# Six modulation units of layer 1 behind layer 0's last expert, and two result buffers in place of four

## The reference

```
h  = rms(x, attn_norm_g) * (1 + sc1) + sh1          # and hc from the context
y  = attention(h, hc)                               # 8 global heads, 8 local ones with sink
x  = x + g1 * (y @ w_out[l])
h  = rms(x, ffn_norm_g) * (1 + sc2) + sh2
x  = x + g2 * top2_experts(h)                       # 16 experts, in layer 0 for 512 tokens
```

## Time and profile before

| what | us |
|---|---|
| median of 3 runs (lowest to highest) | 1102.76 (1098.95 to 1102.98) |
| the profiled execution, its own time | 1102.94 |
| its span | 1101.0 |
| attention of layer 0 | 156 to 291 |
| experts of layer 0 | 407 to 653 |
| combine | 665 to 691 |
| attention of layer 1 | 765 to 828 |
| experts of layer 1 | 884 to 1095 |

### The profile page before, as it was taken

The page is one execution under the profiler, slowest core; times in us unless marked ns, Lnnn a source line. Parts: engine busy times, 40 slices in busy tenths (PEclk is TensorE's granted clock), DMA queues, the critical chain, the costliest instruction groups (busy, mean ns, idle before and its releaser), DMA issues. The chain is left out here.

```text
span 1101.0 us, 24722 instructions
## 1 busy us (share of the span) xinstructions
PE 934.9 (85%) x9667; PEld 584.8 (53%) x9668; DVE 486.4 (44%) x1375; ACT 299.0 (27%) x678; POOL 51.1 (5%) x71
## 2 busy tenths in 40 slices
PE   4679999899897789999999853799989787999975
PEld 2234465443343755666766533487658654555543
DVE  1416666566513543333333314386871543343422
ACT  3312235455301431111111102423770311122111
POOL 1000000000000001111111113000000000000000
PEclk9889999999898689999999976899999799999988
DMA  8995039879802104999999997302403359999995
GB/s 320 420 395 176 1 136 426 310 283 424 350 5 108 46 1 163 397 418 417 418 418 418 420 413 276 133 1 78 171 1 153 153 236 428 428 428 416 414 430 232
DMA packets 33905, 299.05 MB, mean 272 GB/s; under 512 B 9681, under 2 KB 11105, under 8 KB 16961
## 3 DMA queue, kind: packets, MB, share of 16 engines
q1 hardware_dynamic: 23264, 286.15, 63.4%
q0 software_dynamic: 8880, 12.01, 3.3%
q10 hardware_dynamic: 1712, 0.23, 0.1%
HBM read 289.51 MB, written 16.65 MB: 278 GB/s over the span
## 5 line engine op out<-in xcount | busy, mean ns | idle before, releaser
L730 PE MATMUL bank<-ring,rows_buf 128*32 128x256 f32 x4160 | 248.3, 392 | 54.5 <-DMA ring<-in_w_up_dram 27.4
L730 PEld LDWEIGHTS bank<-ring,rows_buf 128*32 128x32 f32 x4160 | 157.3, 113 | 138.8 <-issue 72.6
L503 PE MATMUL bank<-rows_buf,ring 128*128 128x512 f32 (+1 forms) x320 | 119.3, 528 | 12.5 <-ACT rows_buf L898 6.5
L742 PE MATMUL bank<-ring,rows_buf 128*32 128x256 f32 x2080 | 125.7, 380 | 1.2 <-ACT work L1010 1.2
L503 PEld LDWEIGHTS bank<-rows_buf,ring 128*128 128x128 f32 x320 | 63.2, 198 | 61.7 <-issue 48.2
L742 PEld LDWEIGHTS bank<-ring,rows_buf 128*32 128x32 f32 x2080 | 73.4, 110 | 41.6 <-issue 7.6
L1440 DVE COPY rows_buf<-rows_buf x176 | 52.3, 297 | 87.0 <-DVE rows_buf L1440 45.8
L603 PE MATMUL bank<-rows_buf,ring 128*128 128x512 f32 (+1 forms) x256 | 86.4, 501 | 1.0 <-DVE rows_buf L1223 1.0
L1179 DVE RECIPROCAL work<-work 128x512 f32<-128x512 f32 (+1 forms) x20 | 54.3, 2713 | 68.8 <-ACT work L908 68.8
L1201 DVE TENSOR_REDUCE rows_buf<-bank 128x1 f32<-128x512 f32 (+1 forms) x96 | 57.4, 598 | 44.8 <-PE bank L544 22.9
L603 PEld LDWEIGHTS bank<-rows_buf,ring 128*128 128x128 f32 x256 | 49.8, 196 | 37.7 <-issue 32.0
(11 more groups left out here) (228 smaller groups left out, 1059.8 us busy)
## 6 DMA issues: line engine op xcount, KB each, us to landing
ring<-in_w_gate_dram SPq DMA_DIRECT2D x32, 2048.0 KB, 15.0
ring<-in_w_up_dram SPq DMA_DIRECT2D x32, 2048.0 KB, 19.8
ring<-in_w_down_dram SPq DMA_DIRECT2D x32, 2048.0 KB, 19.0
ring<-in_ada_w_dram SPq DMA_DIRECT2D x24, 2048.0 KB, 10.3
ring<-in_w_in_dram SPq DMA_DIRECT2D x8, 1536.0 KB, 27.7
y_rows<-in_table_dram SPq DMA_DIRECT2D x1, 8704.0 KB, 59.9
ring<-in_w_out_dram SPq DMA_DIRECT2D x4, 2048.0 KB, 10.2
y_rows<-work POOLq DMA_DIRECT2D x44, 128.0 KB, 10.6
```

The lines of the kernel that those rows point to most:

```text
L503: last = mm(bank[1 + i % 2][:, 0:widths[i]], qk_weights(i, k), h_t[:, k, 0:widths[i]], start=(k == 0), stop=(k == KD - 1))
L730: last = mm(o.rearrange("r (s c i) -> r s c i", s=2, c=KF), hc_t[l][:, k, :], w[:, :, k, :, CHUNK * q:CHUNK * q + CHUNK], start=(k == 0), ...
L742: last = mm(bank[4][CHUNK * q:CHUNK * q + CHUNK, 0:256], he_t[l][:, k, :], wd[:, k, 256 * q:256 * q + 256], start=(k == 0), stop=(k == KF ...
```

## The change

`LATE = 18`: units 4 to 17 stay in attention of layer 0, now one behind every fourth head, in groups 4 to 11 and 12 to 17. Units 18 to 22 run on PE between the last `down` of layer 0 and the first turn of `combine`, unit 23 behind the turn of tile 1, and their turn behind the last tile's sums. Their loads are issued behind expert 14 (slots 6 to 8) and behind expert 15 (slots 0 to 2). The first half of layer 1's w_out waits for unit 18, and expert 0 of layer 1 also for unit 23. DVE sums the late group and makes its gains behind the scaling of layer 1's first norm. The wide, spaced copy of silu(c) that units need is made a second time, in `work` (`late_wide`), just ahead of the expert loop. For that `work` loses two of the four result buffers, so `row_out(g)` now waits for the store of piece g-2 instead of g-4, and POOL's loop steps by two.

The diff, without the hunks that only declare semaphores or follow the number of buffers elsewhere:

```diff
-ADA_GROUPS = [(0, 1), (1, 2), (2, 3), (3, 4), (4, 12), (12, 24)]
+ADA_GROUPS = [(0, 1), (1, 2), (2, 3), (3, 4), (4, 12), (12, 18), (18, 24)]
+LATE = 18
+LATE_MODS = 4 * LATE
...
         y_t = tokm[:, :, :].rearrange("p t n -> p (t n)").rearrange("p (k n) -> p k n", k=KD)
+        late_wide = [work[:, 264 + 504 * i:512 + 504 * i].rearrange("p (k c) -> p k c", k=4) for i in range(2)]
+        late_parts = ring[:, 8, 3584:4096]
         smx = h_t[:, 4, 0:64]
...
         hc_t = [a.rearrange("p (k r) -> p k r", k=KD) for a in hc_flat]
-        act_g = [work[:, 1288:1416], hflat[:, 1024:1152]]
+        act_g = [work[:, 1280:1408], hflat[:, 1024:1152]]
         he = [spare[:, 0:128], hflat[:, 1152:1280]]
...
         pos = work[:, 736:744]
-        y_out0 = [work[:, 264 + 256 * i:520 + 256 * i] for i in range(4)]
+        y_out0 = [work[:, 512 + 512 * i:768 + 512 * i] for i in range(2)]
         less_b = work[:, 0:64].bitcast(BF16).rearrange("p (s t e) -> p s t e", s=2, t=4)
...
                 load_expert(0, 0, 0, (part,))
-            for u in range(4, 24):
+            for u in range(4, LATE):
                 if u == 5:
...
                 if l == 0:
-                    sp.wait_ge(ada_used, 21)
+                    sp.wait_ge(ada_used, 17)
                     load_wout(0, 0)
-                    sp.wait_ge(ada_used, 22)
+                    sp.wait_ge(ada_used, 18)
                     load_wout(0, 1)
-                    sp.wait_ge(ada_used, 24)
                 else:
...
                     sp.wait_ge(down_mm[0], end_of(sp, 0, 14) + 1)
-                    load_wout(1, 0)
+                    for i in range(3):
+                        load_ada(6 + i, LATE + i, late_in[i])
                     total = all_chunks(sp, 0)
                     sp.wait_ge(down_mm[0], total + 1)
+                    for i in range(3):
+                        load_ada(i, LATE + 3 + i, late_in[3 + i])
                     sp.wait_ge(fills_done, 2)
                     sp.dma_start(spare, table[:, C_BLK:C_G]).then_inc(cst_in, 16)
+                    sp.wait_ge(ada_used, LATE + 1)
+                    load_wout(1, 0)
                     sp.wait_ge(yg_in[3], 32)
+                    sp.wait_ge(ada_used, 24)
                     load_expert(1, 0, 0)
...
                     pe.wait_ge(ada_in[u], 16)
-                else:
+                elif u < LATE:
                     s = (6, 3, 4, 5)[u % 4]
                     pe.wait_ge(ada2_in[u % 4], 16 * (u // 4))
+                else:
+                    s = (6, 7, 8, 0, 1, 2)[u - LATE]
+                    pe.wait_ge(late_in[u - LATE], 16)
                 n = [u0 <= u < u1 for u0, u1 in ADA_GROUPS].index(True)
...
                     pe.wait_ge(ada_summed, n)
-                    pe.wait_ge(scv_spaced, 1)
+                    pe.wait_ge(scv_spaced, 1 if u < LATE else 2)
                 elif u == u0 and n > 0:
...
                         first_col = 30 - 2 * (u - u0)
-                        last = mm(bank[7][32 * q:32 * q + 32, :], scv_wide[:, k, first_col:first_col + 32], w[:, k, :],
+                        wide = scv_wide[:, k] if u < LATE else late_wide[k // 4][:, k % 4]
+                        last = mm(bank[7][32 * q:32 * q + 32, :], wide[:, first_col:first_col + 32], w[:, k, :],
                                   start=(u == u0 and k < 4), stop=(u == u1 - 1 and k >= 4))
...
                     pe.wait_ge(ada_summed, n)
+                rows = parts if ADA_GROUPS[n][0] < LATE else late_parts
                 for m in range(4):
-                    last = turn(ada_bank(n)[:, P * m:P * m + P], parts[:, P * m:P * m + P], ident)
+                    last = turn(ada_bank(n)[:, P * m:P * m + P], rows[:, P * m:P * m + P], ident)
                 last.then_inc(ada_turned, 1)
...
                     pe.wait_ge(qk_done, 10 * l + i - 1)
+                if (l, i) == (1, 1):
+                    pe.wait_ge(ada_summed, len(ADA_GROUPS))
                 mm(bank[(3, 0)[i % 2]][:, 0:n], head_ones, sq[i % 2][:, 0:n], start=True, stop=True)
...
                     for i in (n, n + 1):
-                        if l == 0 and i in (24, 60):
-                            ada_turn(4 if i == 24 else 5)
+                        if l == 0 and i in (32, 56):
+                            ada_turn(4 if i == 32 else 5)
                     if 2 <= n < UNITS[l] + 2:
...
                     for i in (n, n + 1):
-                        if l == 0 and i % 3 == 1 and i < 60:
-                            ada_unit(4 + i // 3)
+                        if l == 0 and i % 4 == 1 and 4 + i // 4 < LATE:
+                            ada_unit(4 + i // 4)
...
                 tb = sum(TOK_TILES[:l])
+                for u in range(LATE, 23):
+                    ada_unit(u)
                 for tt in range(nt):
...
                     last.then_inc(c_turned, 1)
+                    if tt == 1:
+                        ada_unit(23)
                     if l == 0 and tt >= 2:
...
                     tile_sums(nt - 1)
+                ada_turn(6)
...
                     act.wait_ge(ada_turned, n)
-                do(parts, bank[7][:, :], ACT.Identity).then_inc(parts_ready, 1)
+                do(parts if n < 6 else late_parts, bank[7][:, :], ACT.Identity).then_inc(parts_ready, 1)
...
                         probs_out(n - 2)
-                    if l == 0 and n in (22, 58):
-                        ada_parts(4 if n == 22 else 5)
+                    if l == 0 and n in (30, 54):
+                        ada_parts(4 if n == 30 else 5)
...
                     act.wait_ge(down_mm[l], g + 2)
-                    act.wait_ge(rows_stored[0], (g + 4) // 4 * 16)
-                    act.wait_ge(rows_stored[1], (g + 7) // 4 * 16)
-                    act.wait_ge(rows_stored[2], (g + 6) // 4 * 16)
-                    act.wait_ge(rows_stored[3], (g + 5) // 4 * 16)
-                    nc.scalar.copy(work[:, bass.ds(g % 4 * 256 + 264, 256)], bank[4][:, 0:256]).then_inc(rows_ready, 1)
+                    act.wait_ge(rows_stored[0], (g + 2) // 2 * 16)
+                    act.wait_ge(rows_stored[1], (g + 3) // 2 * 16)
+                    nc.scalar.copy(work[:, bass.ds(g % 2 * 512 + 512, 256)], bank[4][:, 0:256]).then_inc(rows_ready, 1)
...
                     act.wait_ge(rows_ready, total + 1)
-                    act.sem_inc(rows_ready, 3)
+                    act.sem_inc(rows_ready, 1)
                 else:
...
                     tile_squares(3)
+                ada_parts(6)
...
                 total = all_chunks(pool, l)
-                with pool.Fori(0, (total + 3) // 4) as m:
-                    for i in range(4):
-                        pool.wait_ge(rows_ready, 4 * m + i + 2)
-                        pool.dma_start(y_rows[bass.ds(4 * CHUNK * m + CHUNK * i, CHUNK), :].rearrange("r (q c) -> q r c", q=4),
+                with pool.Fori(0, (total + 1) // 2) as m:
+                    for i in range(2):
+                        pool.wait_ge(rows_ready, 2 * m + i + 2)
+                        pool.dma_start(y_rows[bass.ds(2 * CHUNK * m + CHUNK * i, CHUNK), :].rearrange("r (q c) -> q r c", q=4),
                                        y_out0[i]).then_inc(rows_stored[i], 16)
                 pool.wait_ge(pos_ready, l + 1)
-                pool.wait_ge(rows_stored[0], (total + 7) // 4 * 16)
-                for i in range(1, 4):
-                    pool.wait_ge(rows_stored[i], (total + 11) // 4 * 16)
+                pool.wait_ge(rows_stored[0], (total + 3) // 2 * 16)
+                pool.wait_ge(rows_stored[1], (total + 5) // 2 * 16)
                 pool.sem_inc(fills_done, 1)
...
             def add_bias(m0, m1):
-                dve.wait_ge(ada_summed, 4 if m1 == 2 * KD else len(ADA_GROUPS))
+                dve.wait_ge(ada_summed, {2 * KD: 4, LATE_MODS: 6, DEPTH * NMOD: 7}[m1])
                 bias = vec[:, V_ADAB + m0:V_ADAB + m1].unsqueeze(2).to_broadcast([P, m1 - m0, 2])
...
                         y_out(n // 4 - 1)
-                    if l == 0 and n in (25, 61):
-                        ada_sum(4 if n == 25 else 5)
+                    if l == 0 and n in (33, 57):
+                        ada_sum(4 if n == 33 else 5)
...
                 fill_window(1)
+                for i in range(2):
+                    link(v.memset(late_wide[i], 0.0))
+                    copied = v.tensor_copy(late_wide[i][:, :, 30:32], scv[:, 4 * i:4 * i + 4, :])
+                copied.then_inc(scv_spaced, 1)
                 total = all_chunks(dve, 0)
...
                 norm_scale(2 * l, 512)
+                if l > 0:
+                    ada_sum(6)
+                    add_bias(LATE_MODS, DEPTH * NMOD)
+                    gains(1, (1,))
                 qk_norms(l)
...
                 if l == 0:
-                    add_bias(2 * KD, DEPTH * NMOD)
-                    gains(0)
-                    gains(1)
+                    add_bias(2 * KD, LATE_MODS)
+                    gains(0, (0, 1))
+                    gains(1, (0,))
```

(12 more changed lines are left out.)

## The result

The changed kernel takes 1104.36 us (median of 20 runs, 1098.86 to 1110.34) where the kernel before takes 1099.17 (median of 20, of which the three runs shown ahead of the prediction are a part; two of them, 1113.91 and 5240.49, were slow and stand outside the ratio). The ratio is 1.0049, 95% interval 1.0032 to 1.0066: slower by about 5.4 us. The prediction had the sign. Of the 11 us between 1115 and 1104.36, 3.8 are in the starting point: the sum began at the profiled execution's 1102.94, and the median of the kernel before is 1099.17.

A forecast was written before the change was run, and what follows sets the result against it. The prediction took PE and the DMA engines to bound the kernel in turn, stage by stage. Attention -9.0, ring +2 and combine +19.5 gave +12.5 us on 1102.94, so 1115, range 1105 to 1122.

The forecast's parts named there:

- Attention: Attention of layer 0: six units leave it, gaining 9.0 us, between 7.5 and 11.5.
- The ticks of the two halves: Attention's values steps of four heads: 512 keys gain 3.8 us, 256 keys 4.8, from ticks that lose a unit.
- the one with the stall: Attention, ahead of the second group's first unit: PE's 2.52 us idle time moves but stays; 0.4 us gained.
- the price of a unit beside 256 keys: Attention's half with 256 keys: 1.9 or 0.9 us from two units to one, 2.0 for two ticks losing their only one.
- The ring: Experts of layer 0: two result buffers instead of four make copies wait for stores; +2 us, between 0 and 8.
- Combine: Combine of layer 0: six late loads and units in front of the turns; +19.5 us, between 17.5 and 22.
- The first turn: Combine: first turn of results some 35 us behind the last down step, in place of 22.
- the sums: Combine: tile 3's sums end 55 to 60 us behind the last down step, instead of 38.
- the two ends: Combine: gathers served first, sums done at 709 to 710.5; or gathers last, beside the loads, 709 to 713.5.
- rival 1: Combine: loads hidden, only unit 23's 1.9 us shows, store ring hidden too; -7.1 us, 1096; chance 0.07.
- rival 3: Experts of layer 0: late copies starve the refills, 8 to 10 us in place of 2; 1121 to 1123; chance 0.12.
- Rival 2: Loads partly hidden: attention gains 11.5, ring costs nothing, combine costs 12 to 14; 1102 to 1106 us; chance 0.11.

The follow-up runs named there:

- spread_three: Kernel before with three late units, three result buffers, filling stores at once, seventeen units spread evenly over layer 0's attention: 1079.62 us against 1097.56, ratio 0.9827.

## Why the prediction was right or wrong

**What is missing from the sum.** The step that failed is the list of what the change touches. The prediction said that two buffers cost a wait in the expert loop, and followed the buffers' semaphores only there. The same semaphores are brought to their starting value by the chain of stores at the start, and the change cuts that chain from seven stores to three. The change has it in one line, the waits of the kernel before name it (15.5 us of ACT), and no term of the sum speaks of it: it put at nothing what is a gain of over 7 us. It is worth -7.6 us (the kernel with the stores at once; -9.2 in the profiled pair). With that term the sum would have been +4.9, and +5.4 was measured. That they agree so well is in part luck: attention gave 2.4 us more than foretold, and some 2 us of the medians, the other way, are not placed (below).

**Attention: mechanism right, size low.** Foretold -9.0, between 7.5 and 11.5; measured -11.4. The ticks of the two halves were counted rightly, and the one with the stall is as foretold: it moved (2.52 us of idle time before, 2.23 after, the unit cold both times). The cold unit isn't a constant, though: in the kernel with only the ring changed the same 2.52 us of idle time left that unit at 1.92 us. What failed is the price of a unit beside 256 keys. I took the 6.63 us of one tick for the cost of one unit; it is the cost of one unit badly placed. In the changed kernel, with a unit in every tick, they take 5.63 each, as some ticks before the change already did. So the even order gives the full 1.9 for each unit taken out where one stays, the tick of 6.63, which kept its one unit, falls to 5.63 as well, and the two last ticks, which lost theirs, give 1.65 and 0.77. That place counts is shown by the seventeen units of spread_three (-6.4 us, of which the stall's 2.5 us and the 1.3 that its cold unit took longer would be 3.8).

**The ring: right.** Foretold +2 (0 to 8); +2.3 in the stage of the pair and 2.2 from the medians, which alone could not tell it from nothing. The copies were late as reckoned, and PE's wait for the last experts' weights took up most of the delay, 8.5 us of new waits against 7.5 of old ones.

**Combine: right.** Foretold +19.5 (17.5 to 22), measured +20.2. The first turn stands 33.7 us behind the last down step (foretold 35), the sums 58.3 (foretold 55 to 60). Of the two ends it is the second: the gathers come last. They share the engines with queued loads and land after 24.7 us in place of 6.1, and they start 13.6 us behind the last down step in place of 11.7, as the last store before them takes 10.3 us to land in place of 7.7. The first turn's last wait, 1.56 us, is for DVE's sum of the gathered rows, and with no units in front of it it stands where it stood. The late loads alone make the difference (37.8 us without them).

**The rest of the two traces.** The output projection's stage is 3.2 us shorter after the change, though nothing of it was changed. The windows of 6 us around its start (291.0 before, 269.9 after) show where:

```profile
289.00:295.00 6.00, 5.15 (x13) 2.33 (x14) 2.06 (x10) 0.28 (x1) 0.00 (x0) 0.60 1.01 401
```

```profile
268.00:274.00 6.00, 5.18 (x18) 2.43 (x19) 1.66 (x8) 0.24 (x1) 0.00 (x0) 1.00 0.60 199
```

The granted clock is 0.60 of full speed in the one and 1.00 in the other, and the output projection's matmuls take 58.2 us from first to last before and 55.2 after: such a cold start is 3 us. Whether the change has a part in it isn't shown. The kernel before with its stores at once has the long time too (58.2), but the one with only the ring changed takes 55.9, and the changed kernel with its stores at once 57.3. The medians come near the stages: from the kernel with only the ring changed (-5.4) to the changed kernel (+5.4) are 10.8 us for the moved units, while the stages give +20.2 - 11.4 = 8.8; the remaining 2 us are not placed.

**The rivals.** The loads are not hidden (rival 1): the fifth piece's unit stands at 659.85, 32 us behind the last down step's start, and the first turn at 665.05. The ring is not the larger cost (rival 3). Rival 2, a result of 1102 to 1106, came closest in size and had one of its three terms right, attention's full 11.5; its other two fell (the ring cost something, and combine 20.2 and not 12 to 14), and its total came out only by the saving that it overlooked too.

## What to carry to other kernels

Before you cost a smaller or larger ring, list every place where its semaphores are waited for or brought to their starting value, and read who waits there; here the start was worth over three times the loop (7.6 us against some 2). Idle time of an engine is only a hole if the loads of the work put there fit as well: ask what stands in the load queue beside the transfer that the chain waits for, since even a load that nobody is waiting for delays it. Work that fills another engine's latency should be spread evenly and never put in the same step as the result that it needs.

## What the runs showed of the hardware

Beside a queue full of 2 MB loads, gathers of 512 KB from another queue rose from a landing time of 6.1 us to 24.7, while the engines moved 421 GB/s in all: they took four times as long though they were issued 1.27 us apart as before. With fewer loads beside them they took 19.9 us (without w_out's 2 MB) and 9.6 (without the six pieces). The Trainium skill (DMA: Bandwidth & Descriptors, Queues, rings and completion order) lets each engine go round its queues packet by packet. That the gathers land late beside the loads agrees with it; how the engines split their time no run here measures. And 5.6 us of matmuls put into an idle time of 6 us did not only fit there, they left PE at full clock: the next 16 matmuls of 512 columns took 7.1 us, and the first 32 behind an idle 6 us 16.8. A short idle time need not end the same way twice: behind 2.52 us of it the same 16 matmuls took 3.2 us in four of the profiled executions and 1.92 in a fifth.
